# One tile earlier: copies and sums of the turned rows in an output projection's pipeline

## The reference

```python
mixed = jnp.concatenate([out_a, out_b], axis=-1) @ w_out[l]
x = x + rms_norm(mixed, norm_mix_post[l])
h = rms_norm(x, norm_ffn_pre[l])
f = (jax.nn.silu(h @ w_gate[l]) * (h @ w_up[l])) @ w_down[l]
```

## Time and profile before

| | |
|---|---|
| median of 3 runs | 2493.77 us (2493.25 to 2494.11) |
| the profiled execution, its own time | 2494.11 us |
| its span, first to last instruction | 2492.3 us |
| mean granted TensorE clock | 0.987 of full |
| the output projection's steady part | about 1041 to 1230 us of the span |

### The profile page before, as it was taken

One profiled execution on the slowest core, in us unless ns is written; L12 is line 12 of the kernel. 1 busy time (PEld: TensorE's weight loads), 2 busy tenths in 40 slices (PEclk: granted clock), 3 DMA queues, 4 the chain that ended last, 5 costly groups with the idle time before them and its releaser, 6 DMA issues.

```text
span 2492.3 us, 34874 instructions
## 1 busy us (share of the span) xinstructions
PE 2359.2 (95%) x11796; PEld 1965.9 (79%) x11796; DVE 1645.7 (66%) x3089; ACT 1198.8 (48%) x2731; POOL 703.0 (28%) x818
## 2 busy tenths in 40 slices
PE   8999989996888888799999999999999999999998
PEld 7888877884777777688788888888888888888886
DVE  6777776554888898345765565557686455465877
ACT  5566664333676676434533333345554333334444
POOL 2333342222576675365410111110001111111001
PEclk9999999998999999899999999999999999999999
DMA  5121123334232221568643223266763332326774
GB/s 188 43 58 58 58 72 114 136 122 155 61 103 84 76 84 33 198 198 271 234 149 107 102 98 114 89 199 224 260 237 124 117 107 93 106 91 246 238 261 148
DMA packets 222352, 340.08 MB, mean 136 GB/s; under 512 B 20576, under 2 KB 119904, under 8 KB 220384
## 3 DMA queue, kind: packets, MB, share of 16 engines
q1 hardware_dynamic: 222176, 337.86, 40.5%
HBM read 234.50 MB, written 103.28 MB: 136 GB/s over the span
## 4 chain that ended last, share of the span: by engine, by line
PE 57%; DVE 1%; DMA 0%; issue 0%; ACT 0%; POOL 0%; SPq 0%; POOLq 0%; ACTq 0%; DVEq 0%
PE ff_psum L2466 33%; PE ff_psum L2490 16%; PE ff_psum L1739 6%; PE ff_psum L1753 1%; DMA ff_hop<-hop_s 0%; PE ff_psum L1724 0%; DMA op_w_raw<-in_w_out_dram 0%; DVE ff_y L2423 0%; DVE op_h_row L1676 0%; DVE ff_y L2327 0%; DVE ff_hop L1692 0%; ACT ff_hop L2097 0%; DVE ff_y L2270 0%; POOL ff_ss L2073 0%; ACT ff_junk L2208 0%
## 5 line engine op out<-in xcount | busy, mean ns | idle before, releaser
L2466 PE MATMUL ff_psum<-ff_hop,ff_a_hi 128*128 128x512 f32 x2464 | 760.4, 390 | 5.6 <-DVE ff_hop L2226 4.0
L2466 PEld LDWEIGHTS ff_psum<-ff_hop,ff_a_hi 128*128 128x128 f32 x2464 | 462.8, 188 | 103.2 <-issue 6.8
L2466 PE MATMUL ff_psum<-ff_hop,ff_a_lo 128*128 128x512 f32 x1232 | 480.0, 390 | 0.0
L2466 PEld LDWEIGHTS ff_psum<-ff_hop,ff_a_lo 128*128 128x128 f32 x1232 | 231.6, 188 | 48.0
L2490 PE MATMUL ff_psum<-ff_a_hi 128*128 128x512 f32 x604 | 235.0, 389 | 0.0
L2490 PE MATMUL ff_psum<-ff_a_lo,ff_a_hi 128*128 128x512 f32 x604 | 235.0, 389 | 0.0
L2490 PE MATMUL ff_psum<-ff_a_hi,ff_a_lo 128*128 128x512 f32 x604 | 235.0, 389 | 0.0
L2092 ACT ACTIVATE ff_a_hi<-ff_w_raw 128x512 fp32r<-128x512 f32 x220 | 137.8, 628 | 194.9 <-PE ff_psum L2466 191.0
L1224 ACT ACTIVATE da_probs<-da_psum,da_bias 128x512 f32<-128x512 f32 (+3 forms) x320 | 196.1, 622 | 64.2 <-DVE da_bias L1276 59.6
L2219 DVE TENSOR_TENSOR ff_a_lo<-ff_w_raw,ff_a_hi 128x512 fp32r<-128x512 f32 x220 | 162.3, 739 | 90.6 <-ACT ff_a_hi L2092 90.6
L2047 POOL TENSOR_TENSOR ff_go<-ff_go 128x512 f32<-128x512 f32 x22 | 28.4, 1292 | 656.2 <-DVE ff_go L2300 635.0
(11 more groups left out here) (238 smaller groups left out, 5090.5 us busy)
## 6 DMA issues: line engine op xcount, KB each, us to landing
g_s<-ff_go SPq DMA_DIRECT2D x154, 256.0 KB, 2.0
ff_ring<-g_s SPq DMA_DIRECT2D x154, 256.0 KB, 2.9
ff_ring<-in_w_down_dram SPq DMA_DIRECT2D x132, 256.0 KB, 3.2
ff_w_raw<-in_w_gate_dram SPq DMA_DIRECT2D x44, 512.0 KB, 3.4
ff_w_raw<-in_w_up_dram SPq DMA_DIRECT2D x44, 512.0 KB, 3.5
pp_x<-in_x_dram SPq DMA_DIRECT2D x32, 512.0 KB, 4.3
ff_hop<-hop_s SPq DMA_DIRECT2D x14, 1024.0 KB, 7.9
hop_s<-op_odd SPq DMA_DIRECT2D x8, 1280.0 KB, 5.8
```

Source lines behind the costliest of these rows:

```text
L2466: last = pe.matmul(ps[:, bank, :], w[:, unit % R, at], hop[i][:, h, c, :], start=(i in (0, 1, 6) and c == 0 and x_ == 0), stop=(c == 3 and ...
```

## The change

Four calls move in the loops of `OutProj`. `copy_h` on ACT takes tile k - 1 instead of k - 2 and stands after `square_x`. `first_sums` on DVE and `second_sums` on POOL run at even k for tile k - 1 instead of at odd k for tile k - 2; `first_sums` moves from behind `norm_y` to behind `norm_x`. On SP the store takes tile k - 1 instead of k - 2. The work and TensorE's program stay the same.

```diff
             if k >= 1:
                 self.square_y(act, k - 1)
-            if k >= 2:
-                self.copy_h(act, k - 2)
             if k + 1 < TILES:
                 self.hi_m(act, k + 1)
             if k >= 1:
                 self.square_x(act, k - 1)
+            if 1 <= k < TILES - 1:
+                self.copy_h(act, k - 1)
...
             if k >= 1:
                 self.norm_y(dve, k - 1)
-            if k >= 3 and k % 2 == 1:
-                self.first_sums(dve, k - 2)
             if k + 1 < TILES:
                 self.lo_m(dve, k + 1)
             if k >= 1:
                 self.norm_x(dve, k - 1)
+            if k >= 2 and k % 2 == 0:
+                self.first_sums(dve, k - 1)
...
-            if k >= 3 and k % 2 == 1:
-                self.second_sums(pool, k - 2)
+            if k >= 2 and k % 2 == 0:
+                self.second_sums(pool, k - 1)
...
-            if k >= 2:
-                (self.store_even if k % 2 == 0 else self.store_odd)(sp, k - 2)
+            if 1 <= k < TILES - 1:
+                (self.store_even if k % 2 == 1 else self.store_odd)(sp, k - 1)
```

## The result

The changed kernel takes 2508.72 us (median of 6 runs, 2507.3 to 2510.15), the kernel before 2493.97 (6 runs, 2493.25 to 2495.75): a ratio of 1.0057, 95% interval 1.0045 to 1.007. It is slower, by 14.75 us or 0.6% between the medians; forecast were 2509.5 us and 15.7. The profiled execution took 2507.67 us with a span of 2505.9, 13.6 over the span before.

The account below looks back on a forecast made before the run. TensorE, 95% busy, was taken to bound the kernel, so late chains make it wait: 8.5 + 0.35 + 3.3 + 2.35 + 1.2 = 15.7 us on the median 2493.77 gives 2509.5 us, range 2500 to 2517.

Parts of the forecast that it names:

- The even beats: Output projection, tiles 2, 4, 6, 8, 10: TensorE waits 1.7 us before each turn_h, 8.5 us in all.
- H + 5.3: Even beats: POOL's y_rstd starts 5.3 us after the start of turn_h on TensorE, behind second_sums.
- The lock: SBUF operations of DVE and POOL take turns, so sums don't overlap; rival that it isn't met or slack is larger: 0.12.
- Tiles 11 and 12: FFN preparation now stands between copies and squares or ahead of norm_y: waits of 0.35 and 3.3 us.
- Tile 13: Hop half and three pairs of sums ahead of norm_y: a wait of 2.8 where 0.45 stood, +2.35 us.
- the beat after it: Tile 14: its chain is late, but TensorE runs the last tile and two FFN products first: 0 us.
- the rival of the clock: TensorE's granted clock falls after waits of 1.7 to 3.3 us: two hits add 4 us, all seven 15; chance 0.09.
- Into the FFN: Tile 15: norm_y 3.2 us later, mostly absorbed by a load wait; TensorE's wait moves by 1.2 us, bounds 0 and 3.
- the tail gives back: Rival at FFN entry: tile 13's store leaves before the first hop load, waits shrink by 3 us; no loss, chance 0.06.
- 0.6 us of slack: Odd tiles: the copies delay norm_y to 4.16 us after turn_h starts, against a deadline of 4.76, at no cost.

Follow-up runs that it names:

- sums-alone kernel: Against the kernel before, only first_sums (DVE) and second_sums (POOL) moved one tile earlier; copies and stores stayed: 2506.95 us.
- the copies alone: Against the kernel before, only ACT's copy_h moved, to tile k-1 after square_x; sums and stores stayed: 2508.76 us.
- wait ladder: The kernel before with norm_x of tiles 1, 3, 5, 7 and 9 repeated in whole or half rows, so TensorE idles for growing lengths: 2514.52 us, one run.
- last pair early: The kernel before with copies, sums and store of tile 13 alone moved early, to k = 14: 2493.31 us against 2493.69 in the same set.

## Why the prediction was right, and where its terms were off

The forecast was 2509.5 us, and 2508.72 was measured; the mechanism in the body was the one described. The sum, 15.7, came out at 13.6 in the trace, with errors of both signs.

**The even beats (8.5 forecast, 6.9 measured).** The places were right: waits in every even tile, none in odd ones, y_rstd at H + 3.0 in odd beats (1071.62 - 1068.61 = 3.01). The size was 1.38 per tile instead of 1.7. Of the 0.33 between H + 5.3 and H + 4.97, 0.24 is T3: I had it start when T1 is over, at H + 2.04, and it started at 1082.75 = H + 1.80, 0.16 us before T1's recorded end, at its full 1.30. T2 was then held by T3 as forecast (1.59 us instead of 0.7, ending 0.55 after it). The sums-alone kernel showed that POOL's order alone makes 1.34 of it, and the kernel with the second sums behind y_rstd that it goes with that order. The other 0.4 us of the 7.29 are 0.04 to 0.09 in each of the five odd beats.

**The lock.** Rows 6 had carried it, and it held for T2. I had not followed it to norm_x, which T3 held for 1.02 us in the kernel before already. In the changed kernel T3 is gone from there, so the forecast did not suffer. For the copies alone I did count norm_x, but not add_x and `split_swa`, which are stretched in the same way by 0.3 and 0.5 us.

**Tiles 11 and 12 (0.35 and 3.3).** Measured 0.36 and 3.12. Taking the preparation out of the way took the first to 0.01 over an odd beat and left 1.64 over it in the second.

**Tile 13 (2.35 forecast, 2.98 measured) and the beat after it (0 forecast, 1.62).** Here the rival of the clock happened, in its mild form. norm_y was forecast for H + 7.55 and started at 1208.83 = H + 8.34, because the transposes came at the lower clock: the second copy started at 1202.50 = H + 2.01 instead of H + 1.2, and the sums stand behind it. The wait of 2.01 us that followed brought the second stretch of low clock: 13.46 instead of 11.84 to the first FFN product. But that loss did not all last. TensorE came 1.6 us later to the product that waits for ACT's `ff_s`, and the wait there shrank from 0.99 to 0.18, so 0.8 of it was paid back. I gave the clock 0.09 and priced it at 2 us a hit, from 2.1 for the stretch of rows 2. That was too much: a mean of 0.64 between full and half clock over 4.5 us is a loss of 1.6. In this kernel it was 0.6 in the one beat, and 1.6 in the other before the repayment. What I had written for this stage, a granted clock of 1.00, was wrong: it was 0.98 up to the FFN's entry, with 0.50 and 0.59 in the two stretches.

**Into the FFN (+1.2 forecast; from turn_h(13) to the end -0.39 measured, the +1.62 and -2.01 of the table).** The step of the chain was nearly right: square_x of tile 15 was forecast for H + 22.3 and started at 1238.22 = H + 21.9, and the product that waits for ACT came 0.82 later behind turn_h(13) than before. How much of this 0.82 is the chain's and how much the clock's no run separates. But I counted only the chain and left the load's part to a rival. The store of tile 13 left at 1222.59 and the hop loads at 1229.99, 7.4 us apart instead of 0.41, ACT's wait fell from 4.67 to 1.32, and the second wait of TensorE, for the next hop, from 3.98 to 2.75. So the rival "the tail gives back" came true by about 1.2 us, but not in its full 2491, since the body's slack did not hold. The kernels with that store early or late on an otherwise equal body differ by 4.9 us in the trace and 5.2 in the median. But there the late store also made the hop loads leave 3.7 us later, which the changed kernel's queue doesn't; for the changed kernel the cause rests on one trace.

The errors were -1.2 us in the first ten beats, +0.6 at tile 13 and -1.6 from turn_h(13) on; the small ones elsewhere nearly cancel, and together they make the 2.1 between 15.7 and 13.6. The medians lie 14.75 apart and not 13.6, because the profiled execution of the changed kernel ran 1.05 us below its median. That the forecast of 2509.5 came within 0.8 us of 2508.72 is in part luck: it was closer than its working. That it was slower at all rests on the part that was shown: POOL's second sums hold y_rstd back by 2 us more than the copies do, where the copies had left 0.6 us of slack in the chain.

## What to carry to other kernels

When background work is moved, count for each engine what it puts ahead of the latency chain's next step, and compare it with the slack to the beat; moves on two engines need not add up. Look for slack where a chain is shown without cover, as tile 13 was here. If waits of about 2 us and more come out, price the lower clock with them, and ask whether a later wait will pay it back. For each store that moves ask which load it now stands ahead of, and whether that load must wait in the queue until the store's data is ready.

## What the runs showed of the hardware

- A DVE operation with its inputs in SBUF is held by a POOL operation for that operation's whole length, also a scalar_tensor_tensor: norm_x took 2.30 us beside T3 and 1.28 without it. The same kind of operation with its large input in PSUM was not held (norm_y, 1.41 us beside T3).
- A hand-over can come before the recorded end: T3 began 0.16 us before T1's end in the record, at full speed.
- TensorE lost clock after idling for 1.91 us (wait ladder) and 2.01 us (changed kernel), 1.6 us each time, and did not after 2.45 (wait ladder) and 2.98 (last pair early). The same wait of 2.75 us was followed by 0.69 in one kernel and by 1.00 in another.
- At the FFN's entry the full clock was worth little: with 1.00 behind the wait instead of 0.64 the way to the end was 0.2 us shorter, and a new wait of 1.39 us came up (last pair early).
- The hop loads take longer right behind a 1.28 MB store. In the seven kernels with the store 0.4 to 1.9 us ahead of them, ACT's first hop half began 7.5 to 8.6 us after their issue; in the five with the store 5.3 to 7.4 us ahead it was 4.7 to 5.1.
